# Gate/up projection of a decoder layer: a fourth k-pair as a seven-product block, and two subtractions moved to GpSimd

## What is computed

```python
h = rms_norm(x, ffn_norm)
return x + (jax.nn.silu(h @ w_gate) * (h @ w_up)) @ w_down     # w_gate, w_up: 2048 x 5632, w_down: 5632 x 2048
```

## Time and profile before

| | us |
|---|---|
| median of three runs | 1110.25 |
| profiled execution, its own time | 1111.72 |
| its span | 1110.0 |
| PE busy | 1097.8 (99%) |
| DVE busy | 757.1 (68%) |
| ACT busy | 570.1 (51%) |
| POOL busy | 36.9 (3%) |

### The profile page before, as it was taken

One profiled execution on the slowest core, in us unless ns is written; L12 is line 12 of the kernel. 1 busy time (PEld: TensorE's weight loads), 2 busy tenths in 40 slices (PEclk: granted clock), 3 DMA queues, 4 the chain that ended last, 5 costly groups with the idle time before them and its releaser, 6 DMA issues.

```text
span 1110.0 us, 13577 instructions
## 1 busy us (share of the span) xinstructions
PE 1097.8 (99%) x5191; PEld 913.8 (82%) x5191; DVE 757.1 (68%) x674; ACT 570.1 (51%) x571; POOL 36.9 (3%) x44
## 2 busy tenths in 40 slices
PE   9999999999999999999999999999999999999997
PEld 6788889997888888888888888888888888888886
DVE  6444458664576798898898898898887654444444
ACT  6644346656655555454554555555554433334444
POOL 0390000000000000000000000000000000000000
PEclk9999999999999999999999999999999999999999
DMA  9755544653445555555555555556555655555552
GB/s 346 258 189 190 193 140 132 198 182 115 150 155 189 185 194 195 193 202 205 189 192 198 212 191 189 201 190 213 189 189 206 221 198 200 195 190 189 189 190 113
DMA packets 58316, 212.42 MB, mean 191 GB/s; under 512 B 4017, under 2 KB 11953, under 8 KB 41009
## 3 DMA queue, kind: packets, MB, share of 16 engines
q1 hardware_dynamic: 56288, 206.58, 54.2%
q10 hardware_dynamic: 2000, 5.46, 1.4%
HBM read 209.93 MB, written 2.10 MB: 191 GB/s over the span
## 4 chain that ended last, share of the span: by engine, by line
PE 96%; DMA 2%; ACT 1%; DVE 1%; issue 0%; SPq 0%; DVEq 0%; ACTq 0%
PE ps L1413 63%; PE ps L1189 9%; PE ps L1191 9%; PE ps L1190 9%; PE ps L1228 2%; DMA raw<-in_w_in 2%; PE ps L1276 1%; PE ps L1377 1%; PE ps L1379 1%; PE ps L1378 1%; PE ps L1275 0%; ACT w_hi L404 0%; ACT junk L431 0%; DVE w_lo L782 0%; PE ps L1247 0%
## 5 line engine op out<-in xcount | busy, mean ns | idle before, releaser
L1413 PE MATMUL ps<-w_hi,xp_hi 128*128 128x512 f32 x539 | 211.7, 393 | 0.0
L1413 PE MATMUL ps<-w_hi,xp_lo 128*128 128x512 f32 x539 | 209.9, 389 | 0.0
L1413 PE MATMUL ps<-w_lo,xp_hi 128*128 128x512 f32 x539 | 209.7, 389 | 0.0
L1105 DVE TENSOR_TENSOR w_lo<-raw,w_hi 128x2048 fp32r<-128x2048 f32 x44 | 100.8, 2291 | 108.6 <-ACT w_hi L700 108.6
L700 ACT ACTIVATE w_hi<-raw 128x2048 fp32r<-128x2048 f32 x44 | 84.4, 1917 | 136.9 <-DMA raw<-in_w_down 136.9
L782 DVE TENSOR_TENSOR w_lo<-raw,w_hi 128x2048 fp32r<-128x2048 f32 (+2 forms) x44 | 91.9, 2088 | 88.7 <-ACT w_hi L404 88.7
L974 DVE TENSOR_TENSOR w_lo<-raw,w_hi 128x2048 fp32r<-128x2048 f32 x55 | 125.7, 2286 | 34.7 <-ACT w_hi L616 34.7
L616 ACT ACTIVATE w_hi<-raw 128x2048 fp32r<-128x2048 f32 x55 | 105.0, 1909 | 62.9 <-DMA raw<-in_w_gu 62.9
L1413 PE MATMUL ps<-w_hi,dx_hi 128*128 128x512 f32 x352 | 137.0, 389 | 0.0
L1413 PE MATMUL ps<-w_hi,dx_lo 128*128 128x512 f32 x352 | 136.9, 389 | 0.0
L1413 PE MATMUL ps<-w_lo,dx_hi 128*128 128x512 f32 x352 | 136.9, 389 | 0.0
(11 more groups left out here) (216 smaller groups left out, 1681.5 us busy)
## 6 DMA issues: line engine op xcount, KB each, us to landing
raw<-in_w_gu SPq DMA_DIRECT2D x88, 1024.0 KB, 4.8
raw<-in_w_down SPq DMA_DIRECT2D x44, 1024.0 KB, 4.8
raw<-in_w_in SPq DMA_DIRECT2D x34, 1024.0 KB, 5.1
raw<-in_w_out SPq DMA_DIRECT2D x16, 1024.0 KB, 5.1
raw<-in_w_in SPq DMA_DIRECT2D x8, 576.0 KB, 3.8
raw<-in_w_ukv SPq DMA_DIRECT2D x3, 1024.0 KB, 5.3
raw<-in_w_uq SPq DMA_DIRECT2D x3, 768.0 KB, 4.5
xT_raw<-in_xT SPq DMA_DIRECT2D x4, 512.0 KB, 8.1
```

The source lines that it names most:

```text
L1105: nc.vector.tensor_tensor(w_lo[n % 4][:], raw[n % 4][:], w_hi[n % 4][:].bitcast(F32), ALU.subtract).then_inc(lo_ready, 1)
L1413: mm = nc.tensor.matmul(out, x, wt, start=start and j + m == 0, stop=stop and 3 * j + m == n - 1, skip_group_check=resumed)
```

## The change

`SUMS` becomes (0, 2, 4, 5): chunk 5 is a seven-product chunk too. Chunks 1 and 3 stay plain, but their low parts are subtracted by POOL, in a new loop at the end of its program (22 instructions of 128x2048), signalled to PE by a new semaphore `lo_pool`. DVE keeps the low parts of the plain chunks 6 and 7. `mix_sums` and half 0 of the mixing move from step 4 to step 5, half 0 waits for the middle of chunk 6, half 1 for its end, and PE needs them in chunk 7. In DVE's order half 1 now stands between the sums and the low parts of the next block's chunk 0. The sums of chunk 5 wait for PE to finish chunk 2, whose buffer of sums they take. The activations of pair 5 are prepared as seven blocks instead of two, which also moves the tensor `hid` 3 KB up. The order of the four groups in chunk 7 changes so that both gate banks come first.

```diff
-SUMS = (0, 2, 4)
+SUMS = (0, 2, 4, 5)
 NS = len(SUMS)
+BY_POOL = (1, 3)
+ND = FB - len(BY_POOL)
...
-for _step, _pairs in ((58, (0, 1)), (59, (2, 3)), (62, (4, 5)), (FF0, (6, 7))):
+for _step, _pairs in ((58, (0, 1)), (59, (2, 3)), (62, (4,)), (63, (5,)), (FF0, (6, 7))):
...
+            for i in range(FS):
+                for p in BY_POOL:
+                    n = FF0 + i * FB + p
+                    pool.wait_ge(hi_ready, n + 1)
+                    nc.gpsimd.tensor_tensor(w_lo[n % 4][:], raw[n % 4][:], w_hi[n % 4][:].bitcast(F32),
+                                            ALU.subtract).then_inc(lo_pool, 1)
...
-                    if p == 4:
+                    if p == SUMS[-1]:
                         act.wait_ge(mix_done, i * 2 + 1)
...
-                            act.wait_ge(ffn_done, i * 3 + (2 * b + 1))
+                            act.wait_ge(ffn_done, i * 3 + (b + 1))
...
+                if p in BY_POOL:
+                    return
...
+                    if p == SUMS[-1]:
+                        dve.wait_ge(chunk_used, i * FB + (FF0 + SUMS[1] + 1))
...
-                    dve.wait_ge(chunk_used, i * FB + (FF0 + 6))
+                    dve.wait_ge(chunk_used, i * FB + (FF0 + 7))
...
-                    if p == 4:
+                    if p == SUMS[-1]:
                         mix_sums(i)
                         mix_banks(i, 0)
-                    if p == 5:
-                        mix_banks(i, 1)
...
+                    elif p == SUMS[-1]:
+                        prep_lo(i, p + AHEAD, "s")
+                        mix_banks(i, 1)
+                        prep_lo(i, p + AHEAD, "l")
...
-                sides = ((0, 0), (1, 0), (0, 1), (1, 1)) if p in (5, 6) else ((0, 0), (0, 1), (1, 0), (1, 1))
+                sides = ((0, 0), (1, 0), (0, 1), (1, 1)) if p > SUMS[-1] else ((0, 0), (0, 1), (1, 0), (1, 1))
...
-                    if p == 6 and g % 2 == 0:
+                    if p == SUMS[-1] + 2 and g % 2 == 0:
                         pe_.wait_ge(mixed, i * 2 + (g // 2 + 1))
...
-                    if p == 5 and g == 1:
+                    if p == SUMS[-1] + 1 and g == 1:
                         mm.then_inc(part_done, 1)
...
-                    pe_.wait_ge(lo_ready, i * FB + (FF0 + p + 1))
+                    if p in BY_POOL:
+                        pe_.wait_ge(lo_pool, i * len(BY_POOL) + (BY_POOL.index(p) + 1))
+                    else:
+                        pe_.wait_ge(lo_ready, i * ND + (FF0 + sum(q not in BY_POOL for q in range(p + 1))))
```

More of the change, by code:

```diff
@@ L89 @@
 put(54, ("yt", 6), ("yt", 7))
-for _step, _pairs in ((58, (0, 1)), (59, (2, 3)), (62, (4, 5)), (FF0, (6, 7))):
+for _step, _pairs in ((58, (0, 1)), (59, (2, 3)), (62, (4,)), (63, (5,)), (FF0, (6, 7))):
     put(_step, *(("xs2" if _pair in SUMS else "xt2", _pair) for _pair in _pairs))
-XS_SPLIT = {59: 0, 60: 1, 63: 2}
+XS_SPLIT = {59: 0, 60: 1, 63: 2, 64: 3}
 MID = 51
@@ L131, in build @@
             offset += 2 * size
-        H0 = 153 * K
+        H0 = 156 * K
         assert offset <= H0
@@ L257, in build @@
         sum_step, tops_hi = sem("sum_step"), sem("tops_hi")
+        lo_pool = sem("lo_pool")
         mix_done, mix_first, mix_step = sem("mix_done"), sem("mix_first"), sem("mix_step")
@@ L1126, in ffn @@
                             if b == 0:
-                                dve.wait_ge(ffn_done, i * 3 + 2)
+                                dve.wait_ge(ffn_done, i * 3 + 3)
                             else:
@@ L1440, in sums_chunk @@
                     if first and not late:
-                        after(unit_act, "a", ("xt2", 5))
-                        after(unit_dve, "v", ("xt2", 5))
+                        after(unit_act, "a", ("xs2", 5))
+                        after(unit_dve, "v", ("xt2", 3))
                     elif not first:
@@ L1487, in plain_chunk @@
                                [xp_lo[p][:, j, toks] for j in range(2)], [w_hi[slot][:, j, :] for j in cols],
-                               [w_lo[slot][:, j, :] for j in cols], p == 1 and g == 3, p in (5, FB - 1), resumed=p > 5)
-                    if p == 5 and g == 1:
+                               [w_lo[slot][:, j, :] for j in cols], p == 1 and g == 3, p > SUMS[-1], resumed=p == SUMS[-1] + 2)
+                    if p == SUMS[-1] + 1 and g == 1:
                         mm.then_inc(part_done, 1)
@@ L1516, in down_ready @@
             def down_ready(i, k):
-                pe_.wait_ge(lo_ready, i * 4 + (DN0 + k + 1))
+                pe_.wait_ge(lo_ready, i * 4 + (FF0 + FS * ND + k + 1))
                 pe_.wait_ge(dx_made, i * 4 + (k + 1))
```

## The result

| | before | with the change |
|---|---|---|
| median, us | 1110.61 (4 runs) | 1159.88 (4 runs, 1159.69 to 1160.5) |
| span of the profiled execution | 1110.0 | 1157.9 |

The change makes the kernel 4.4% slower: the ratio is 1.0443, with a 95% interval of 1.043 to 1.0456. That is +49.3 us, where the prediction had 1148.5 us, +38. (The median of before contains one run more than the three shown ahead of the prediction.)

The account below looks back on a forecast made before the run. PE was taken as the bound, with DVE close behind in gate/up. Blocks of 46.2 instead of 42.5 us gave +37 over ten, -0.7 for the last, +2 for the first: +38.3, so 1148.5 us, range 1114 to 1166.

Parts of the forecast that it names:

- the main case: Whole kernel: the summed forecast of 1148.5 us, with 1140 to 1156 us given chance 0.50.
- rival 1: Block boundary: POOL holds DVE back more, e.g. ahead of `t_lo`, making chunk 0' late; 1156 to 1165 us, chance 0.15.
- The gain on PE: Chunk 5 in gate/up: 24 to 21 matmuls in 11 blocks, 0.68 us a block, 7.5 us in all.
- Term 1: Block boundary: DVE's chain from `part_done` to `t_lo` takes 9.75 us against PE's 8.4; PE stands 1.3 us.
- Term 2: Block boundary: POOL's 4.5 us subtraction locks SBUF reads, delays DVE's sums; PE waits 2.9 us at the second hidden turn.
- PE's clock: Gate/up: a granted clock under nine tenths was named as a cost not counted; no size given.
- the start: First gate/up block: DVE is already full and POOL's two blocks fall on it; +2 us (0 to 5).
- The sum of a block: Gate/up block: 42.5 - 0.7 + 1.3 + 2.9 + 0.2 = 46.2 us.
- Rival 3: Block boundary: no blocking by POOL, only the mixing chain's wait; 43.1 us a block, 1116 us, chance 0.10.
- Rival 4: Block boundary: faster, if the `part_done` to `t_lo` chain is under 9.1 us and POOL doesn't block; 1103 to 1108, chance 0.10.

Follow-up runs that it names:

- e5: Changed kernel with POOL only filling the low parts of chunks 1 and 3 with zeros, and next chunk 0's sums ahead of mixing half 0: 1113.21 us.
- e10: Changed kernel with only chunk 7's low part on POOL, next chunk 0's sums ahead of mixing half 0, first `keep_hidden` ahead of chunk 2's `t_hi`: 1112.42 us.
- e3: Changed kernel with the three sums of the next chunk 0 moved on DVE ahead of the first half of `mix_banks`: 1198.33 us.
- e9: Kernel before the change (three seven-product chunks, old mixing order) with the low part of chunk 7 alone on POOL: 1110.27 us, ratio 0.9994.
- e2: Changed kernel with POOL filling the low parts of chunks 1 and 3 with zeros instead of subtracting, these left out of the product: 1114.91 us.
- e8: Kernel before the change (three seven-product chunks, old mixing order) with the low parts of chunks 1 and 3 on POOL: 1120.8 us, ratio 1.009.
- e1: Changed kernel with the low parts of chunks 1 and 3 back on DVE, four seven-product chunks kept, POOL idle: 1134.28 us.

## Why the prediction was right, point by point

**Direction and range: right, with luck in it.** 1159.88 lies in 1114 to 1166, and 49.3 us against a forecast of 38 is the same way and less than a third more. But the main case, 1140 to 1156, had a chance of 0.50 and was missed. The time lies where rival 1 (1156 to 1165, chance 0.15) had put it, and that rival's mechanism, POOL ahead of `t_lo` at the boundary, did not occur in this kernel.

**The gain on PE: right.** 33 matmuls are gone, 0.68 us a block. e5 and e10 show that they don't become time as long as DVE is late for what PE needs next.

**Term 1: right in mechanism, 1.3 us predicted, 0.98 measured.** The chain from half 0 to PE was 8.95 us (620.88 to 629.83) where the prediction added 9.3 for this part. From the first sum to half 1 it took 2.59 us (622.02 to 624.61), not the 2.79 of sums followed by `w_lo`. From `w_lo` to `t_lo` it took 1.66 (625.75 to 627.41), not the 1.87 of the earlier trace rows; in the kernel before, `t_lo` starts as ACT's `t_hi` ends (643.87 + 1.92 = 645.79), while here `t_hi` is done ahead of `w_lo`'s end. So the 1.87 held a wait for ACT that the sum took for DVE's own time. What I had not seen is that the order doesn't matter much (e5).

**Term 2: right.** The price of a subtraction, 4.5 us from a 128x192 row and the fixed part of one-input instructions, is 4.60 to 4.63 where nothing was in its way (e3, e9). The reading was put at 4.3 and DVE lost 3.1 us at `t_sum` (4.33 for 1.22) where 3.0 were predicted; the turn waited 2.63 us instead of 2.9. Filling in place of subtracting costs DVE nothing (e2), and a subtraction beside DVE instructions with one operand in PSUM costs it nothing either (e9); what costs is the overlap with DVE instructions that read two operands from SBUF. The rule of the Trainium skill in SBUF — State Buffer, section "SBUF: two separate sides", an exclusive lock for the whole instruction, agrees with these rows: DVE was held for 4.3 of POOL's 4.6 us. The prediction's own evidence that DVE waits was thin: the POOL instruction beside DVE's at 57.83 is one of 0.69 us with one input (it starts at 57.79 and is not in the earlier trace rows), and DVE lost 0.16 us to it.

**The mis-sized terms: PE's clock, put at nothing, and the start, put at 2 us.** The sum of a block, 46.2 us, took PE's clock as given. In the two blocks in which the clock stayed up it is right to 0.2 us (46.00 and 45.97). In the other eight the clock fell behind the stand at the turn and slowed PE by 1.7 us; seven of them last 47.0 to 47.2, the eighth is the last one, without a boundary. The prediction names a fall of the clock among the things that would show it incomplete, but put no price on it. The profiled span is 47.9 us longer, where the sum had 38.3. With the wait at the first boundary counted to the blocks, the ten blocks are longer by 44.0 us in place of 37, that is 7.0 of the 9.6 us that are missing. The start cost 4.7 us instead of 2 (5.0 until the first turn, less that boundary's 1.0, plus the 0.7 that chunk 5 had saved); this lies within the prediction's 0 to 5, and the rows at 392 to 400 us show it: POOL held DVE's `xp_lo`, PE stood 3.0 us, and its clock fell there too. In e2, where POOL only fills, the same `xp_lo` takes 1.09 us (394.38) and the first turn comes at 442.70, 0.3 us later than before. Behind the last turn nothing differs by more than 0.2 us.

**Rivals.** Rival 1, that POOL gets in ahead of `t_lo`, did not happen here but did in e3, after one move on DVE, at 1198 us. Rival 3 is e2. Rival 4 needed a boundary chain under 9.1 us and no blocking; e5 removes the blocking and the wait for `t_lo` and still isn't faster, so its condition was too generous: half 0 of the mixing has a due time too. That the range holds the result owes something to its upper end, taken from rival 1 and not from the clock.

## What to carry to other kernels

Before work is moved to POOL, don't compare sums of busy times: look at which DVE instructions will run beside it. Where they read two operands from SBUF, nearly all of POOL's duration (4.3 of 4.6 us here) is added to the one that comes second, and what counts is who waits for that one; where they read PSUM, or DVE waits for someone else, the same work was free (e9). A product saved on the busiest engine is worth nothing if the engine behind it has to do as much between two of its due times as there is time, and its mean load of 88% doesn't show that.

## What the runs showed of the hardware

- A waiting POOL gets in at the next boundary of DVE's instructions, even one without an idle gap in the profile. In e8 the POOL instruction that starts at 622.00, while DVE is in a `t_sum`, has its turn ahead of the DVE instruction at 622.26, which then takes 4.98 us instead of 0.69. In e3 a lead of 0.07 us decided who waited.
- POOL filling 128x2048 took 1.81 to 1.83 us and disturbed no DVE instruction beside it, whereas a subtraction of the same size took 4.60 to 4.63 and held DVE for about 4.3. Beside the same subtraction DVE's instructions with one operand in PSUM kept their 1.23 us (e9).
- PE's waits of 0.8 us at the boundary left the granted clock at 1.00, and so did e1's at the turn (1.6 us). Behind the changed kernel's waits at the turn, 2.5 us each, it fell to 0.50 in eight of ten blocks, with matmuls that started 0.43 us apart, and stayed at 1.00 in two. Filling the stand with useless matmuls made the kernel 7.6 us faster.
